# The join of w_o and the up projection: four tiles on each side computed in two token parts

## What is computed

```python
h = rms_norm(xp, norm_mix_pre[l])
qa, ka, va, qr, kr, vr, gr, ga, gb = mixer_inputs(h, pos_p, w_in[l])
...
m = jax.nn.sigmoid(ga) * ya + jax.nn.sigmoid(gb) * yr
return m @ w_o
...
def block_tail(x, mix, g_mix_post, g_ffn_pre, g_ffn_post, w_up, w_down):
    x = x + rms_norm(mix, g_mix_post)
    h = rms_norm(x, g_ffn_pre)
    f = jnp.square(jax.nn.relu(h @ w_up)) @ w_down
    return x + rms_norm(f, g_ffn_post)
```

## Time and profile before

| | |
|---|---|
| median of 3 runs | 900.01 us (899.95 to 902.49) |
| profiled execution | 901.57 us, span 899.7 us |
| TensorE matmul busy | 876.5 us (97%) |
| TensorE weight load busy | 858.3 us (95%) |
| VectorE busy | 468.2 us (52%) |
| ScalarE busy | 302.2 us (34%) |
| GpSimd busy | 57.9 us (6%) |
| mean granted clock of TensorE | 0.983 |

### The profile page before, as it was taken

How to read it: one execution, slowest core, us unless ns; L and a number is a source line. 1 busy time by engine, 2 the same in 40 slices (tenths; PEclk the granted TensorE clock), 3 DMA queues, 4 the chain that set the end, 5 groups by cost and what they waited for, 6 DMA issues and landing times.

```text
span 899.7 us, 16798 instructions
## 1 busy us (share of the span) xinstructions
PE 876.5 (97%) x6908; PEld 858.3 (95%) x6908; DVE 468.2 (52%) x741; ACT 302.2 (34%) x444; POOL 57.9 (6%) x49
## 2 busy tenths in 40 slices
PE   6999999999999999999996999999999999999997
PEld 6999999999999999999995899999999999999995
DVE  6323667666786677666338543334433443334336
ACT  5211546444531111454324332123312331133322
POOL 1000000000000000000435200000000000000223
PEclk9999999999999999999996999999999999999997
DMA  9222212321312131122221122222222222232202
GB/s 299 92 94 93 85 47 83 105 71 58 120 63 85 53 101 54 48 94 94 94 93 48 48 92 70 75 93 93 94 94 93 92 68 75 91 95 93 94 1 100
DMA packets 78456, 77.28 MB, mean 86 GB/s; under 512 B 2944, under 2 KB 76304, under 8 KB 78416
## 3 DMA queue, kind: packets, MB, share of 16 engines
q1 hardware_dynamic: 69328, 70.53, 24.3%
q10 hardware_dynamic: 8448, 4.02, 1.6%
q0 software_dynamic: 640, 2.17, 0.7%
HBM read 71.70 MB, written 4.99 MB: 85 GB/s over the span
## 4 chain that ended last, share of the span: by engine, by line
PE 94%; DVE 3%; issue 1%; DMA 1%; ACT 1%; SPq 0%; ACTq 0%; DVEq 0%
PE acc L749 78%; PE wk L749 3%; PE wk L773 3%; PE wk L887 3%; DVE scaled L1414 1%; DVE act_lo L1434 1%; PE wk L849 1%; PE wk L848 1%; DMA x_nat<-in_x_prompt 1%; PE wk L956 1%; PE wk L806 1%; PE wk L965 1%; PE wk L797 1%; PE wk L954 0%; PE wk L840 0%
## 5 line engine op out<-in xcount | busy, mean ns | idle before, releaser
L471 ACT ACTIVATE w_hi<-w_raw 128x1024 fp32r<-128x1024 f32 x123 | 130.4, 1060 | 475.8 <-PE acc L749 460.5
L749 PE MATMUL acc<-act_hi,w_hi 128*128 128x272 f32 x1264 | 268.3, 294 | 9.3 <-DVE act_lo L1434 8.6
L749 PE MATMUL acc<-act_hi,w_lo 128*128 128x272 f32 x1264 | 263.9, 290 | 0.0
L749 PE MATMUL acc<-act_lo,w_hi 128*128 128x272 f32 x1264 | 263.1, 290 | 0.0
L749 PEld LDWEIGHTS acc<-act_hi,w_hi 128*128 128x128 f32 x1264 | 200.5, 190 | 14.4 <-DVE act_lo L1434 9.8
L749 PEld LDWEIGHTS acc<-act_lo,w_hi 128*128 128x128 f32 x1264 | 200.9, 191 | 0.0
L749 PEld LDWEIGHTS acc<-act_hi,w_lo 128*128 128x128 f32 x1264 | 199.8, 191 | 0.0
L1113 DVE TENSOR_TENSOR w_lo<-w_raw,w_hi 128x1024 fp32r<-128x1024 f32 x123 | 150.5, 1224 | 36.5 <-ACT w_hi L471 36.3
L749 PE MATMUL acc<-mid_hi,w_hi 128*128 128x272 f32 x608 | 125.4, 287 | 0.0
L749 PE MATMUL acc<-mid_hi,w_lo 128*128 128x272 f32 x608 | 125.0, 288 | 0.0
L749 PE MATMUL acc<-mid_lo,w_hi 128*128 128x272 f32 x608 | 124.8, 287 | 0.0
(11 more groups left out here) (195 smaller groups left out, 778.2 us busy)
## 6 DMA issues: line engine op xcount, KB each, us to landing
w_raw<-in_w_in SPq DMA_DIRECT2D x44, 512.0 KB, 4.4
w_raw<-in_w_ff_up SPq DMA_DIRECT2D x32, 512.0 KB, 4.4
w_raw<-in_w_ff_down SPq DMA_DIRECT2D x32, 512.0 KB, 4.2
w_raw<-in_w_o SPq DMA_DIRECT2D x8, 512.0 KB, 4.3
x_nat<-in_x_prompt SPq DMA_DIRECT2D x4, 512.0 KB, 5.2
w_raw<-in_w_attn_out SPq DMA_DIRECT2D x4, 512.0 KB, 3.5
w_raw<-in_w_ret_out SPq DMA_DIRECT2D x4, 512.0 KB, 4.5
k_cache<-in_cache_attn_k SPq DMA_DIRECT2D x1, 1024.0 KB, 11.7
```

Source lines behind the costliest of these rows:

```text
L471: act.activation(w_hi[:, v % 2], w_raw[:, v // 2, :, P * (v % 2):P * (v % 2) + P], ACT.Copy).then_inc(hi_ready, 1)
L749: ins = pe.matmul(dst[:, n, 0:HALF], w[:, k, :], h[:, k, HALF * n:HALF * n + HALF], start=begin, stop=end)
```

## The change

The first four w_o tiles stay whole. The last four (group 14) are computed for tokens 0 to 255 in all four tiles, and then for the other 288, from four split weight buffers, so that each weight is split once. The norm of the first part is done beside the products of the second: sum at k = 3 of the first tile, spread at k = 1 of the second. The first four up tiles (group 15) run in two parts in the same way, into four PSUM places; the sum and spread of the second w_o part lie in the first part of up tiles 0 and 1 (k = 2 and 5), those of the norm over x1 in the last tile of the second part (k = 1 and 5). ScalarE reads w_o's output from PSUM twice, for the square and for y with its gain; VectorE adds the squares. GpSimd adds nothing in this stage. x1 is made by VectorE for two feature tiles at once, both by itself; its squares are added in pairs in `x1_sums`. The root takes scale and epsilon on ScalarE, straight from the summed matmuls in PSUM, here and in the final norm. The final norm's sums wait for both of their inputs before the first matmul.

```diff
--- before.py
+++ after.py
@@ memory and PSUM places
+        eps = place("eps_sb", [P, 8])
+        x1_sums = place("x1_sums", [P, 2, T], at=ends["relu"])
+        w_hi_fourth = place("w_hi_fourth", [P, KT, P], fr, at=work_at)
+        w_lo_fourth = place("w_lo_fourth", [P, KT, P], fr, at=ends["w_hi_fourth"])
+        W_SETS = ((w_hi[:, 0], w_lo[:, 0]), (w_hi_third[:], w_lo_third[:]), (w_hi_fourth[:], w_lo_fourth[:]), (w_hi[:, 1], w_lo[:, 1]))
...
+        MIX_DST = (acc[0], acc[1], wk_halves[1], wk_halves[0])
+        UP_DST = MIX_DST
+        FINAL_SUM = wk[:, SUM_COL:SUM_COL + 5]
+        MIX_SUM = (FINAL_SUM, acc[0][:, 1, 304:309])
+        MIX_RSTD = (256, 512)
@@ GpSimd
-            order.after(pool.memset(sqsum[:], 0.0))
-            for m in range(KT - 1):
-                add_square(1, m)
-
-            pool.wait_ge(sum_mm, 1)
-            order.after(pool.memset(sqsum[:], 0.0))
-            for m in range(KT):
-                if m % 2:
-                    pool.wait_ge(scaled_ready, m // 2 + 1)
-                    pool.tensor_tensor(xT[:, m, :], xT[:, m, :], scaled[:, m % 4, :], ALU.add).then_inc(x1_odd, 1)
-                if m > 1:
-                    add_square(2, m - 2)
-            add_square(2, KT - 2)
@@ ScalarE
+            def root(norm, sums, tiles=range(5)):
+
+                act.wait_ge(sum_mm, norm)
+                prompt = slice(tiles[0], min(tiles[-1] + 1, 4))
+                ins = act.activation(tok_rstd[:, prompt], sums[:, prompt], ACT.Sqrt, scale=1.0 / D, bias=eps[:, 0:1])
...
+            def mix_out(m, part, squares, added):
+
+                s, n = (0, T) if part is None else PARTS[part]
+                src = acc[m % 2][:, :, 0:HALF] if part is None else MIX_DST[m - 4][:, part, 0:n]
...
+                if added:
+                    act.wait_ge(mix_added, added)
+                act.activation(shaped(sq[:, m % 2, s:s + n]), src, ACT.Square).then_inc(mix_sq, 1)
+                act.activation(shaped(y_mix[:, m, s:s + n]), src, ACT.Copy, scale=gains[:, 1, m:m + 1]).then_inc(mix_y, 1)
...
+            def x1_pair(part, p):
+
+                s, n = PARTS[part]
+                act.wait_ge(x1_ready, 4 * part + p + 1)
+                for m in (2 * p, 2 * p + 1):
+                    act.activation(act_hi[:, m, s:s + n], xT[:, m, s:s + n], ACT.Copy, scale=gains[:, 2, m:m + 1]).then_inc(h2_hi, 1)
+                if p == 3:
+
+                    act.wait_ge(x1_added, 3 * part + 1)
+                to = (x1_sums, sq, relu, sq)[p]
+                act.activation(to[:, :, s:s + n], xT[:, 2 * p:2 * p + 2, s:s + n], ACT.Square).then_inc(x1_sq, 1)
+
+            for m in range(4):
+                act.wait_ge(mm_done, 4 * G_WO + m + 1)
+                mix_out(m, None, m, (0, 0, 1, 1)[m])
+                if m < 2:
+                    split_ahead(G_WO, m)
+                if m == 2:
+                    split_set(0, 0, 32 * (G_WO + 2))
+                    split_set(1, 1)
+            split_set(2, 2, 32 * (G_WO + 2))
+            split_set(3, 3)
+            for j in range(4):
+                mix_part(0, j)
+            root(1, MIX_SUM[0], PART_TILES[0])
...
+            mix_part(1, 0)
+            up_set(0)
+            x1_pair(0, 0)
...
+            mix_part(1, 3)
+            root(2, MIX_SUM[1], PART_TILES[1])
+            x1_pair(0, 3)
+            up_set(3)
+            for p in range(4):
+                x1_pair(1, p)
+            split_ahead(G_FFN, 2)
+            root(3, X1_SUM)
@@ TensorE
+            def token_sums(out, sources, tiles=range(5)):
+
+                for t in tiles:
+                    s, n = TILES[t]
+                    for i, src in enumerate(sources):
+                        ins = pe.matmul(out[0:n, t:t + 1], src[:, s:s + n], ones[:, 0:1], start=(i == 0), stop=(i == len(sources) - 1))
                 ins.then_inc(sum_mm, 1)
...
+            for part in range(2):
                 for j in range(4):
...
+                    if part == 0:
+
+                        pe.wait_ge(lo_ready, 4 * G_WO + 4 + j + 1)
+                        if j < 2:
+                            pe.wait_ge(mix_y, 3 + j)
+                    for k in range(KT):
+                        if part and j == 0 and k == 3:
+                            mix_sums(0)
+                        if part and j == 1 and k == 1:
+                            mix_spread(0)
+                        ins = part_products(MIX_DST[j], W_SETS[j], k, mid_hi, mid_lo, part)
+                    ins.then_inc(mm_done if part else mix_mm, 1)
...
+            def second_norm(k):
+                if k == 2:
+                    mix_sums(1)
+                if k == 5:
+                    mix_spread(1)
+
+            def x1_norm(k):
+                if k == 1:
+                    pe.wait_ge(x1_added, 6)
+                    token_sums(X1_SUM, (x1_sums[:, 0, :], x1_sums[:, 1, :]))
+                if k == 5:
+                    spread(3, places=X1_RSTD)
+
+            up_tiles(0, (0, 1), second_norm)
+            up_tiles(0, (2,))
+            up_tiles(0, (3,))
+            up_tiles(1, (0, 1))
+            up_tiles(1, (2,))
+            pe.wait_ge(h2_lo, 2 * KT)
+            up_tiles(1, (3,), x1_norm)
...
+            def final_sums(part):
+
+                pe.wait_ge(sq_added, squares_added(KT - 1 + part))
+                pe.wait_ge(sq_ready, KT + 2 * part)
+                token_sums(FINAL_SUM, (sqsum, sq[:, 1, :]), PART_TILES[part])
@@ VectorE
+            for j in range(3):
+                mix_part_add(0, j)
...
+            def x1_pair(part, p):
+
+                s, n = PARTS[part]
+                b = 2 * (p % 2)
+                if p >= 2:
+                    dve.wait_ge(x1_ready, 4 * part + p - 1)
+                order.after(dve.tensor_tensor(scaled[:, b:b + 2, s:s + n], y_mix[:, 2 * p:2 * p + 2, s:s + n],
+                                              wk[:, MIX_RSTD[part]:MIX_RSTD[part] + n].unsqueeze(1).to_broadcast([P, 2, n]), ALU.mult))
+                dve.tensor_tensor(xT[:, 2 * p:2 * p + 2, s:s + n], xT[:, 2 * p:2 * p + 2, s:s + n], scaled[:, b:b + 2, s:s + n], ALU.add)\
+                    .then_inc(x1_ready, 1)
...
+            norm(1, PART_TILES[0])
+            dve.wait_ge(mix_y, KT)
+            x1_pair(0, 0)
+            x1_pair(0, 1)
+            h2_low(0, 0, 1)
+            mix_part_add(1, 0)
+            split_set(0, 4 * G_FFN, 0)
+            x1_pair(0, 2)
+            h2_low(0, 2, 3)
+            mix_part_add(1, 1)
+            split_set(1, 4 * G_FFN + 1, 1)
+            x1_pair(0, 3)
+            h2_low(0, 4, 5)
+            mix_part_add(1, 2)
+            x1_add(0, 1)
+            h2_low(0, 6, 7)
+            norm_rstd(2, PART_TILES[1])
+            split_set(2, 4 * G_FFN + 2, 2)
...
+            norm_rstd(3)
+            dve.wait_ge(spread_mm, 4)
+            dve.tensor_copy(rstd[:, 0:256], wk[:, 256:512])
+            dve.tensor_copy(rstd[:, 256:512], acc[1][:, 0, 256:512])
+            order.after(dve.tensor_copy(rstd[:, 512:T], X1_RSTD[4]))
...
                     evacuate(0)
+                    split_ahead(g, 2)
                     evacuate(1)
```

More of the change, by code:

```diff
@@ new lines, in mix_part, with split_set @@
+            def mix_part(part, j):
+                if part == 0:
+                    act.wait_ge(mix_mm, j + 1)
+                else:
+                    act.wait_ge(mm_done, 4 * G_WO + 4 + j + 1)
+                mix_out(4 + j, part, 8 + 4 * part + j, ((2, 3, 4, 5), (2, 3, 7, 8))[part][j])
+            def split_set(j, v, load=None):
+                if load is not None:
+                    act.wait_ge(w_in_sem[v // 2], load)
+                act.activation(W_SETS[j][0], w_raw[:, v // 2, :, P * (v % 2):P * (v % 2) + P], ACT.Copy).then_inc(hi_ready, 1)
@@ L681, in up @@
                     g = G_FFN + 4 * c + i
-                    if not (first and j < 2):
+                    if not first:
                         split_ahead(g, j)
@@ new lines, in part_products @@
+            def part_products(dst, w, k, hi, lo, part):
+                s, n = PARTS[part]
+                out = dst[:, part, 0:n]
+                pe.matmul(out, w[0][:, k, :], hi[:, k, s:s + n], start=(k == 0), stop=False)
+                pe.matmul(out, w[0][:, k, :], lo[:, k, s:s + n], start=False, stop=False)
+                return pe.matmul(out, w[1][:, k, :], hi[:, k, s:s + n], start=False, stop=(k == KT - 1))
+            for j in range(4):
+                column_tile(G_WO, j, mid_hi, mid_lo, before=merge_split if j == 0 else None)
@@ new lines, in up_tiles @@
+            def up_tiles(part, tiles, between=None):
+                for k in range(KT):
+                    pe.wait_ge(h2_lo, KT * part + k + 1)
+                    if between:
+                        between(k)
+                    for j in tiles:
+                        if k == 0:
+                            if part == 0:
+                                pe.wait_ge(lo_ready, 4 * G_FFN + j + 1)
```

(45 more changed lines are left out.)

206 lines of the change are left out of this document (91 added, 115 removed).

## The result

The changed kernel takes 890.14 us (median of 4 runs, 887.57 to 891.29), the kernel before, run beside it, 900.46 (4 runs). The ratio is 0.9875, 95% interval 0.9852 to 0.9898. The forecast was 886.8, range 883.5 to 892.0: direction and range held, and the gain is 10.3 us where 13.2 were forecast. The profiled execution took 891.29 (span 889.5), against 901.57 (span 899.7) before.

A forecast was written before the change was run, and what follows sets the result against it. TensorE bounds the kernel almost everywhere, but right after w_o VectorE sets the pace. 15.3 us won in that stage, less 0.5 (tail) and 1.6 (clock), gives 13.2: 900.0 becomes 886.8 us, range 883.5 to 892.0.

The forecast's parts named there:

- VectorE's chain: VectorE's unbroken work from the first w_o part's spread at 464.6: 11.1 us, ending at 475.8.
- ScalarE: In the second w_o part, ScalarE needs 3.1 us per tile against 3.20 of products, so it just keeps pace.
- Weights: Splitting w_o and up weights into four buffer sets hides behind products; up weights there by 459, needed at 464.
- First new wait: TensorE's sum of the second w_o part waits for VectorE's last square add: 0.5 us (0 to 1.5).
- Second new wait: TensorE waits at the second up group for its first low weight half: 1.8 us (1.0 to 2.5).
- The stage: From w_o to the second up group, which starts at 505.75 against 521.05: 15.3 us won.
- The clock: One half-speed stretch of TensorE in the changed kernel costs 1.6 us (0 to 4.8); chance 0.40.
- the three named: Possible half-speed places: wait and sum at 475.4 (0.5 + 1.24), the sum of 2.07, the new wait of 1.8.
- The rival without one: No half-speed stretch in the changed kernel: 885.2 us; chance 0.20.
- the one with two or three: Two or three half-speed stretches in the changed kernel: 888.4 to 890.0 us; chance 0.20.
- The tail: The final norm's last sum waits for both inputs before any matmul: costs 0.5 us (0 to 0.6).

The follow-up runs named there:

- e2: The kernel before, with GpSimd's adds in this stage given to VectorE, in pairs ahead of the low halves: 898.54 us, ratio 0.9973.
- e9: The kernel before, with GpSimd's adds given to VectorE and the x1 adds placed between the low halves: 899.23 us, ratio 0.998.
- e3: The changed kernel with 16 useless GpSimd adds reading SBUF, from the first w_o part's spread on: 904.71 us, ratio 1.004.
- e6: The changed kernel with VectorE's last square add of the second w_o part moved ahead of work that can wait: 888.9 us, single execution.
- e7: The changed kernel with the second up group's first low weight half ahead of the rstd copies, last spread at k = 3: 887.25 us, single execution.
- e10: The changed kernel with the edits of e6 and e7 alone, keeping its own final norm: 884.6 us, ratio 0.9829.
- e4: The changed kernel with 16 useless GpSimd memsets (writes alone) in the same place as e3's adds: 887.86 us, single execution.
- e11: e8 once more, unchanged, beside e10 on the same chip: 882.94 us, ratio 0.9805.
- e1: The changed kernel once more, with no edit: 888.63 us, ratio 0.985.
- e8: The changed kernel with the edits of e5, e6 and e7 together: 883.04 us, ratio 0.9812.
- e5: The changed kernel with the final norm of the kernel before: 889.41 us, ratio 0.987.

## Why the prediction was right, and where it was off

**Direction and mechanism.** Right, and shown: VectorE's passes were long because GpSimd read SBUF beside them (e2 and e9 against e3), and the passage now runs beside w_o's second part. E9 adds what the prediction didn't weigh: taking GpSimd away alone is worth 2 us. No run has the new order with GpSimd's adds kept as they were, so how the 13.2 us of the stage split between the two isn't shown; e3, with a heavier load, lost all of it.

**VectorE's chain.** It was to take 11.1 us from 464.6 (which gives 475.7; the prediction wrote 475.8). With w_o 1.89 us later it would run from 466.5 to 477.7; it ran from 466.66 to 477.80. Low halves were to be 0.48 and about 0.52, and are 0.479 and 0.512.

**ScalarE.** The prices held (0.41, 0.50, 1.06 in after against 0.42, 0.5, 1.06), and nobody on TensorE waited for it in this stage. Weights were hidden as forecast: no wait for one stands in the list before the second group.

**First new wait.** Forecast 0.5, listed as 0.69. Counted from where the next matmul was due at the pace of the last, the gap is 0.85 (477.05 to 477.90). **Second new wait.** Forecast 1.8, listed as 1.51; counted in the same way the gap is 1.67, and VectorE's stretch behind the spread took 2.80 us (506.74 to 509.54) for the 2.9 forecast. E6 and e7 removed each alone, for 0.94 and 1.62 us; together 2.56, which is what e10 shows (81.64 - 79.08).

**The stage.** The second up group was to start at 505.75, with one half-speed stretch at 507.35, and with the late w_o at 509.24. It started at 509.60. Of the 0.36 missing, 0.21 was there at the first sum (477.90, where 475.8 and the late start give 477.69).

**The clock.** One stretch at 1.6 us was the likeliest case; the profile has one, at 1.55. Its place was among the three named, behind the sum of 2.06. That just this case came is in part luck, for the number is not a property of the kernel: in the stage it was 0 in e4, e10 and e11, 1 in after, e1, e6, e7 and e8, and 2 in e5, and e8 and e11 are the same kernel. After's stretch came behind no wait of TensorE since 477.90, so idle time alone doesn't account for it. The rival without one, 885.2, and the one with two or three were as real as the case I took.

**The tail.** The term of the sum that was sized wrong: 0.5 us was forecast (0 to 0.6), 0.95 was measured between square and multiply. The order of work did what was said. TensorE gets to its transposes 1.75 us behind the square's start (874.28 - 872.53) where it had been 1.19, and with the two small steps of VectorE dropped the new order costs 0.37 us at full clock (e6 against e11), inside the forecast. What was left out is the clock: after is 1.33 us above its full-clock value (5.00 against 3.67), before 0.75 above its own (4.05 against 3.30), and the difference, 0.58, is the rest. I counted three places for a fall of the clock and not this one. TensorE now stands idle for 1.73 us in one piece, where it had two waits of 0.53 and 0.36 with a sum between. But e3, e4 and e6 have the same 1.73 us and transposes at full speed (0.66, 0.66 and 0.65 us for four), so the wait by itself doesn't decide it, and the cause stays open.

**The start.** Not in the sum at all: w_o began 1.89 us later in the profiled run, though the change touches nothing before. TensorE alone, 16 to 20 us, of before, after and e10:
```profile
16.00:20.00 4.00, 4.00 (x24) 0.68 1.09 356
```
```profile
16.00:20.00 4.00, 3.97 (x17) 0.50 1.09 356
```
```profile
16.00:20.00 4.00, 4.00 (x34) 1.00 1.09 354
```
The same stretch runs at three clocks, and w_o begins at 424.53, 426.42 and 422.91. It isn't this stretch alone: e5 has it at full clock and begins w_o at 423.66. Over all kernels, before and after alike, it began between 422.91 and 426.42. That this scatter is also what separates the medians (gains of 10.3 and 12.2 us in two sets of runs) is likely and wasn't shown, for only one execution of each kernel was traced.

**Sum.** In the profile: stage -13.2 (forecast -13.7 with the stretch), tail +0.95 (+0.5), start +1.9 (0), the rest +0.2. Of the 3 us by which the profile misses its forecast, 1.9 lie in a start that scattered by 3.5 us over these kernels, then come the stage's 0.5 and the tail's 0.45.

## What to carry to other kernels

Before moving an add from one engine to another, price it on both sides: what the helper takes off, and what its reads of SBUF add to every pass with two SBUF inputs beside it. Here that was a loss per instruction, so short passes suffered most in proportion. When a norm stands between two matmul stages, try cutting the tokens in two and starting the first part's chain under the second part's products: here the whole change took 13.2 us off the stage, and two reorderings inside the passage took about 2 us off the kernel. Then look at what each remaining wait really waits for, and put that one instruction ahead of the ones that can wait: e6 and e7 together took 2.6 us more off the stage, and with the old final norm the kernel takes 883 us. Last, compare stages in traces with the same number of half-speed stretches, or take the stretches out first.
